# One-hot matrices of 128-column comparisons on VectorE, and their products from block 76 on

## The chip, the cores and the metric

One core of a Trainium2 chip runs the whole kernel. The metric is the device time of one execution in microseconds; the kernel before took 1764.61 us (median of 3 runs). TensorE (PE in the profile), VectorE (DVE), ScalarE (ACT), GpSimd (POOL) and SyncE (SP, which here only issues transfers) run their own instruction streams and wait for each other by semaphores.

## The reference

One transformer block over 512 tokens of width 1024: a conditioned projection, an S5 state-space mixer beside a latent attention, an output projection with a layer norm, and then a feed-forward part by product-key experts, with a second layer norm. The expert part is where the change lies:

```python
def token_block(ht):                                  # 128 tokens at a time
    q = (ht @ w_query).reshape(PEER_BLOCK, PEER_HEADS, PEER_QDIM)
    s1 = einsum('thd,hkd->thk', q[..., :128], keys1)   # 8 heads, 128 keys
    s2 = einsum('thd,hkd->thk', q[..., 128:], keys2)
    v1, i1 = top_k(s1, 16);  v2, i2 = top_k(s2, 16)
    top_s, top_c = top_k(all 256 sums v1 + v2, 16)
    e1 = take_along_axis(i1, top_c // 16);  e2 = take_along_axis(i2, top_c % 16)
    expert = e1 * 128 + e2                             # one of 16384
    g = softmax(top_s)
    act = gelu(einsum('thkd,td->thk', u_tab[expert], ht))
    return einsum('thk,thkd->td', g * act, v_tab[expert])
```

So each token takes 8 x 16 = 128 of 16384 experts, each with a weight g, a row of the table u and a row of the table v, 1024 floats each.

## The kernel before

The parts up to the query scores and the first layer norm end at about 552 us. The rest is the function `experts`, and it has two phases.

**The u phase.** The table u is walked in 128 blocks `b` of 128 experts. For the last 384 tokens every block is multiplied in full: SP loads `u_raw` (512 KB) up to four blocks ahead, ACT copies it to its high half `uth` (L1449, three buffers), POOL subtracts to get the low half `utl` (L1428), and PE runs 24 matmuls of 384 columns (`activations`, L1544 to L1546). ACT applies gelu (`acts`, L1461), and SP stores two blocks at a time to DRAM (`store_acts`, L1358). The first 128 tokens go another way: POOL fetches for each of their 128 chosen experts the row of u of every token (`fetch_rows`, L1423, an indirect transfer of 512 KB into a ring of 8 buffers), and DVE takes the dot product (`use_row`, L1629). `row_steps` writes out at which block POOL issues which fetch; a fetch stands in POOL's stream behind that block's `utl`, and waits until the buffer's last row was used.

**Routing.** While this runs, DVE does the top-k of the four token tiles (`topk`, `routing`), with some `use_row` calls between. A tile's softmax exponentials are done by ACT at written-out blocks (`EXP_AT`: 10, 27, 43, 59). The last tile's route is what the third `route_ready` pair tells.

**The one-hot products.** The 384 tokens need a dense matrix of weights g, 128 experts-by-key-1 by 128 by key 2 for every token. With slots (head, choice) on the partitions, a token's matrix is the product of two one-hot matrices: `hot2[slot, key]` is 1 where key = e2, and `hot1[slot, key]` is the weight where key = e1. The weight is kept as two fp16 numbers, high and low, so that there are `hot2`, `hot1h` and `hot1l`, and two matmuls of 128 columns per token. First PE turns the routes (e1, e2, weight; three 128 x 128 transposes for each of three tiles, L1583) so that slots lie on partitions; this stands ahead of block `HOT_FROM` - 2, and waits for `route_ready`. ACT then copies the weights out of PSUM (L1470, L1471). From block `HOT_FROM` = 64 to `HOT_TO` = 120, PE does 96 groups of 4 tokens (`weights_by_token`, L1559 and L1560), each behind the activations of its block; `block_of(n)` spreads them evenly. ACT copies each group's result to `stage` (L1485), and SP stores every 8 groups (2048 KB, L1363) two blocks later.

The one-hot matrices are made in 24 batches of 16 tokens, two buffers each. A call of `hots(m)` on DVE is three `tensor_tensor` instructions of 2048 columns: `hot_eq` = (iota is e1) at L1735, `hot2` = (iota is e2) at L1736, `hot1l` = `hot_eq` x low weight at L1738; e1, e2 and most of the low weights are read from PSUM (banks 6 and 7). The high part is ACT's: `weigh_high` (L1477), 16 activations of 128 columns per batch with the weight as a per-partition scale. DVE starts batch m when the products of batch m - 2 are done (`g_out`). On DVE each batch is followed by three `use_row` calls:

```python
        for m in range(NBATCH):
            hots(m)
            use_rows(3)
        use_rows(12)
```

**The v phase** starts once block 127 is through: the stored gelu values and weights come back, DVE multiplies them (`w_f`, L1748) and splits them (`wl`, L1753), and PE multiplies with the blocks of the table v (L1568 to L1570). It ends with the second layer norm.

Of the kernel before, what the change touches and what calls it, by code (L numbers as in the profile page):

```python
# [8 lines left out]
F16 = mybir.dt.float16  # L9
# [1084 lines left out]
HOT_FROM, HOT_TO = 64, 120  # L1094
# [5 lines left out]
def place_peer(k):  # L1100
# [45 lines left out]
    k.hot_eq = [k.sb(f"hot_eq{i}", hot, 190 + 4 * i, F16) for i in range(2)]  # L1146
    k.iota_b = k.sb("iota_b", hot, 182, F16)
    k.wT = k.sb("wT", [P, TD], 198)
    k.wTh = k.sb("wTh", [P, TD], 199.5, F16)
    k.wTl = k.sb("wTl", [P, P], 200.5, F16)  # L1150
# [139 lines left out]
def row_steps():  # L1290

    steps = [[] for _ in range(2 * NBLK)]
    for j in range(2 * SLOTS):
        if j < 33:
            at = 14 + 1.4 * j
        elif j < 105:
            at = 59 + (j - 33) * 0.777
        elif j < SLOTS:
            at = 115 + (j - 105) * 0.72
        else:  # L1300
            at = NBLK + 5 + (j - SLOTS) * 0.875
# [4 lines left out]
def experts(nc, io, k, ps, out):  # L1306
# [5 lines left out]
    k.hot_ready, k.eq_ready, k.hot1h_done, k.g_out, k.g_evac = k.sems("hot_ready eq_ready hot1h_done g_out g_evac")  # L1312
# [21 lines left out]
    HOT1H_AT = {}  # L1334
    for m in range(NBATCH):
        for half in range(2):
            HOT1H_AT.setdefault(block_of(PER_BATCH * m) - 2 + half, []).append((m, half))
# [6 lines left out]
    e1_at = [ps[:, 6, t * P:(t + 1) * P] for t in range(DT)]  # L1344
    e2_at = [ps[:, 6, TD:512], ps[:, 7, 0:P], ps[:, 7, P:2 * P]]
    w_low = [ps[:, 7, 2 * P:3 * P], ps[:, 7, 3 * P:4 * P], k.wTl[:, :]]
# [67 lines left out]
    def _(pool):  # L1414
# [11 lines left out]
        for b in range(NBLK):  # L1426
# [5 lines left out]
            if b == G_LAST:  # L1432
                pool.wait_ge(k.hot_ready, NBATCH)
                pool.wait_ge(k.hot1h_done, 2 * NBATCH)
# [13 lines left out]
    def _(act):  # L1448
# [18 lines left out]
        def evacuate_weights():  # L1467
# [3 lines left out]
            nc.scalar.activation(k.wT[:, :], src, ACT.Copy, scale=W_UP).then_inc(k.rt_evac, 1)  # L1471

        def weigh_high(m, half):
            act.wait_ge(k.eq_ready, m + 1)
            for i in range(half * BATCH // 2, (half + 1) * BATCH // 2):
                at = m * BATCH + i
                ins = nc.scalar.activation(k.hot1h[m % 2][:, i], k.hot_eq[m % 2][:, i], ACT.Copy, scale=k.wT[:, at:at + 1])  # L1477
            ins.then_inc(k.hot1h_done, 1)
# [24 lines left out]
        for b in range(NBLK):  # L1503
# [8 lines left out]
            for m, half in HOT1H_AT.get(b, ()):  # L1512
                weigh_high(m, half)
# [22 lines left out]
    def _(pe):  # L1536
# [12 lines left out]
        def weights_by_token(n):  # L1549
            m = n // PER_BATCH  # L1550
            if n % PER_BATCH == 0:
                pe.wait_ge(k.hot_ready, m + 1)
                pe.wait_ge(k.hot1h_done, 2 * m + 2)
# [24 lines left out]
        for b in range(NBLK):  # L1578
            if b == HOT_FROM - 2:
                for t in range(DT):  # L1580
                    pe.wait_ge(k.route_ready, 2 * t + 2)
                    for a, dst in enumerate((e1_at[t], e2_at[t], ps[:, 4, t * P:(t + 1) * P])):
                        ins = nc.tensor.transpose(dst, k.route[:, t + 1, a], k.ident[:, :])  # L1583
# [31 lines left out]
    def _(dve):  # L1615
# [111 lines left out]
        def hots(m):  # L1727
            t, i = divmod(m * BATCH, P)
# [148 lines left out]
```

## Time and profile before

| what | value |
|---|---|
| runs of the kernel before | 1765.5, 1764.61, 1758.7 us; median 1764.61 |
| span of the profiled execution | 1759.0 us |
| its own time | not listed apart; it holds the span and the start and end around it |
| u phase | about 552 to 1190 us |
| v phase and last norm | about 1190 to 1759 us |
| PE / DVE / ACT / POOL busy in the span | 1616.7 / 1335.9 / 721.0 / 1028.7 us |

Times in rows are microseconds from the start of the span unless marked ns. An instruction's duration runs past the start of the next where they are pipelined: two that follow each other without a wait start closer together than they last. "x8" merges eight such instructions, and the duration is then that of all eight. What stands in brackets is the idle time of the engine before the instruction, and what ended it. Blocks can be counted by the stores of `acts`, one for every two blocks (1, 3, 5, ...), the first at 564.55 us.

### The profile page before, as it was taken

The page shows a single profiled execution, that of the slowest core. Times are in us where ns is not written, and L with a number is a line of the kernel's source. Part 1 is how long each engine was busy: PE and PEld are TensorE (multiplying, and loading weights), DVE is VectorE, ACT ScalarE, POOL GpSimd, SP SyncE. Part 2 cuts the span into 40 slices and gives each one's busy share as a digit, 9 for nine tenths or more (in the row PEclk, how much of TensorE's full clock was granted, in tenths as well). Part 3 has the DMA queues.
Part 4 walks back from the last instruction along what each step waited for, and adds up shares of the span by engine and source line. Part 5 has one row for each costly group of instructions (what it writes and reads, how often), then busy time and mean ns, then how long its engine had stood idle before and what let it go on. Part 6 is the DMA issues. An engine that isn't in the chain of part 4 may idle for free.

```text
span 1759.0 us, 22141 instructions
## 1 busy us (share of the span) xinstructions
PE 1616.7 (92%) x8149; PEld 1331.2 (76%) x8149; DVE 1335.9 (76%) x2045; ACT 721.0 (41%) x1249; POOL 1028.7 (58%) x622
## 2 busy tenths in 40 slices
PE   3899999997899999997699999997989999999994
PEld 1345576733789999996699999995878888888883
DVE  2494477227424999999988888827889989998997
ACT  2002122420424424332499999933333333333431
POOL 1500164002003578784577778876879988999863
PEclk9898969998999999998899999998999999999997
DMA  7766200361501477784589999998999999999971
GB/s 252 265 229 109 25 3 1 97 215 48 171 21 58 167 258 253 257 280 152 204 333 356 366 353 334 362 388 316 369 354 370 388 375 369 375 385 375 374 273 48
DMA packets 221974, 436.55 MB, mean 248 GB/s; under 512 B 40893, under 2 KB 135722, under 8 KB 220330
## 3 DMA queue, kind: packets, MB, share of 16 engines
q1 hardware_dynamic: 178410, 299.85, 48.8%
q0 software_dynamic: 36864, 134.23, 21.0%
q10 hardware_dynamic: 6592, 1.05, 0.4%
q8 instruction: 65, 1.06, 0.2%
q14 instruction: 43, 0.35, 0.1%
HBM read 377.28 MB, written 56.62 MB: 247 GB/s over the span
## 4 chain that ended last, share of the span: by engine, by line
PE 28%; DVE 20%; DMA 8%; ACT 7%; issue 4%; SPq 1%; POOL 0%; POOLq 0%; DVEq 0%; ACTq 0%
PE ps L1568 8%; PE ps L1569 8%; PE ps L1570 8%; DMA u_raw<-in_peer_uT 5%; ACT hot1h L1477 3%; ACT stage L1485 2%; DVE junk L1629 2%; DMA a_in<-act_scr 2%; DVE eq L1704 2%; ACT uth L1449 1%; DVE eq L1702 1%; DVE wl L1753 1%; DVE cand L1666 1%; DVE route L1705 1%; DVE idx L1664 1%
## 5 line engine op out<-in xcount | busy, mean ns | idle before, releaser
L1428 POOL TENSOR_TENSOR utl<-u_raw,uth 128x1024 fp32r<-128x1024 f32 x128 | 319.6, 2499 | 225.9 <-ACT uth L1449 224.9
L1544 PE MATMUL ps<-h2h,uth 128*128 128x384 f32 x1024 | 352.3, 344 | 16.2 <-POOL utl L1428 12.2
L1545 PE MATMUL ps<-h2l,uth 128*128 128x384 f32 x1024 | 346.5, 338 | 0.0
L1546 PE MATMUL ps<-h2h,utl 128*128 128x384 f32 x1024 | 346.4, 338 | 0.0
L1438 POOL TENSOR_TENSOR vl<-v_raw,vh 128x1024 fp32r<-128x1024 f32 x128 | 311.2, 2432 | 59.6 <-ACT vh L1449 57.8
L1568 PE MATMUL ps<-vh,wh 128*128 128x512 f32 x768 | 302.1, 393 | 16.2 <-DVE wl L1753 13.5
L1569 PE MATMUL ps<-vl,wh 128*128 128x512 f32 x768 | 301.1, 392 | 0.0
L1570 PE MATMUL ps<-vh,wl 128*128 128x512 f32 x768 | 300.8, 392 | 0.0
L1748 DVE TENSOR_TENSOR w_f<-a_in,g_in 128x384 f32<-128x384 f32 x128 | 208.0, 1626 | 58.6 <-DMA a_in<-act_scr 58.0
L1449 ACT ACTIVATE vh<-v_raw 128x1024 fp32r<-128x1024 f32 x128 | 135.4, 1058 | 217.5 <-DMA v_raw<-in_peer_v 175.4
L1544 PEld LDWEIGHTS ps<-h2h,uth 128*128 128x128 f32 x1024 | 195.6, 191 | 18.1 <-POOL utl L1428 13.8
L1545 PEld LDWEIGHTS ps<-h2l,uth 128*128 128x128 f32 x1024 | 195.6, 191 | 0.0
L1546 PEld LDWEIGHTS ps<-h2h,utl 128*128 128x128 f32 x1024 | 195.4, 191 | 0.0
L1568 PEld LDWEIGHTS ps<-vh,wh 128*128 128x128 f32 x768 | 145.4, 189 | 49.9 <-DVE wl L1753 12.2
L1423 POOL DMA_INDIRECT ring<-in_peer_u,row_at x128 | 145.8, 1139 | 54.1 <-DVE dots L1629 26.3
L1570 PEld LDWEIGHTS ps<-vh,wl 128*128 128x128 f32 x768 | 145.6, 190 | 30.6
L1569 PEld LDWEIGHTS ps<-vl,wh 128*128 128x128 f32 x768 | 145.5, 189 | 30.1
L1637 DVE SCALAR_TENSOR_TENSOR ps<-ring,w_sp,ps 128x1024 f32<-128x1024 f32 x127 | 162.3, 1278 | 2.0 <-DVE ps L1637 0.5
L1629 DVE CUSTOM_DVE_ANT_0 junk<-ring,ps 128x1024 bf16<-128x1024 f32 x128 | 149.9, 1213 | 16.3 <-DMA ring<-in_peer_u,row_at 16.2
L1423 POOL DMA_INDIRECT ring<-in_peer_v,row_at x128 | 138.0, 1078 | 22.4 <-issue 19.9
L1449 ACT ACTIVATE uth<-u_raw 128x1024 fp32r<-128x1024 f32 x128 | 135.2, 1058 | 22.3 <-DMA u_raw<-in_peer_uT 21.4
L1753 DVE TENSOR_TENSOR wl<-w_f,wh 128x384 fp32r<-128x384 f32 x128 | 126.0, 984 | 9.0 <-ACT wh L1449 8.8
(345 smaller groups left out, 2480.2 us busy)
## 6 DMA issues: line engine op xcount, KB each, us to landing
u_raw<-in_peer_uT SPq DMA_DIRECT2D x128, 512.0 KB
v_raw<-in_peer_v SPq DMA_DIRECT2D x128, 512.0 KB
w_ada<-in_w_ada SPq DMA_DIRECT2D x12, 2048.0 KB, 9.8
act_scr<-acts SPq DMA_DIRECT2D x64, 384.0 KB
g_scr<-stage SPq DMA_DIRECT2D x12, 2048.0 KB
g_in<-g_scr SPq DMA_DIRECT2D x32, 768.0 KB
a_in<-act_scr SPq DMA_DIRECT2D x64, 384.0 KB
w_q<-in_peer_w_query SPq DMA_DIRECT2D x8, 1024.0 KB, 6.9
```

Source lines behind the costliest of these rows:

```text
L1423: nc.gpsimd.indirect_dma_start(k.ring[j % RING][:, :], None, table, bass.IndirectOffsetOnAxis(ap=k.row_at[:, slot:slot + 1], axis=0)).then ...
L1428: tt(k.utl[b % 3][:, :, :].rearrange(f3), k.u_raw[:, b % 4].rearrange(f3), k.uth[b % 3][:, :, :].bitcast(F32).rearrange(f3), ALU.subtract) ...
L1438: tt(k.vl[:, n % 4], k.v_raw[:, n % 4], k.vh[:, n % 4].bitcast(F32), ALU.subtract).then_inc(k.vl_done, 1)
L1449: copy = lambda dst, src: nc.scalar.activation(dst, src, ACT.Copy)
L1544: mm(o, hi, k.h2h[:, kt, SP:T], start=(kt == 0), stop=False)
L1545: mm(o, hi, k.h2l[:, kt, SP:T], start=False, stop=False)
L1546: ins = mm(o, lo, k.h2h[:, kt, SP:T], start=False, stop=(kt == DK - 1))
L1568: mm(o, hi, k.vh[:, n % 4, cols], start=(n == 0), stop=False)
L1569: mm(o, hi, k.vl[:, n % 4, cols], start=False, stop=False)
L1570: ins = mm(o, lo, k.vh[:, n % 4, cols], start=False, stop=(n == NBLK - 1))
L1629: ins = v.tensor_tensor_reduce(out=k.junk[j % 2][:, :], in0=row, in1=y_sp, scale=1.0, scalar=0.0, op0=ALU.mult, op1=ALU.add, accum_out=k.d ...
L1748: tt(k.w_f[:, n % 2].rearrange("p (c t) -> p c t", t=CHK), k.a_in[:, p % 2, n % 2].rearrange("p (c t) -> p c t", t=CHK), k.g_in[:, q % 2, ...
```

## The change

DVE makes all three matrices itself, token by token. `hots(m)` becomes 48 `tensor_scalar` instructions of 128 columns: `hot2` compares an fp16 iota row with e2 (one per-partition pointer scalar), `hot1h` and `hot1l` compare it with e1 and multiply by the high-scaled weight or the low weight (two pointer scalars each). The scalars are fp32 columns in SBUF: ACT copies e1 and e2 out of PSUM too, and the low weights are one subtraction over 384 columns. `hot_eq`, the replicated iota, `weigh_high` on ACT and the semaphores between them are gone. `HOT_FROM` is 76: transposes ahead of block 74, ACT's copies at its step 73, 96 product groups in 44 blocks, and with them the 12 stores of `stage`. The row fetches 33 to 104 move from block 59 on (0.777 block apart) to block 73 on (0.611 apart), fetches 105 to 127 from block 115 (0.72 apart) to block 117 (0.66 apart).

```diff
--- before.py
+++ after.py
@@ -1091,7 +1091,7 @@
 BATCH = 16
 GROUPS4 = TD // HOTS
 NBATCH = TD // BATCH
-HOT_FROM, HOT_TO = 64, 120
+HOT_FROM, HOT_TO = 76, 120
 SLOTS = PH * PTOP
 RING = 8
 W_UP = 2.0 ** 14
@@ -1143,11 +1143,12 @@
     k.hot2 = [k.sb(f"hot2{i}", hot, at, F16) for i, at in enumerate((78, 82))]
     k.hot1h = [k.sb(f"hot1h{i}", hot, at, F16) for i, at in enumerate((86, 90))]
     k.hot1l = [k.sb(f"hot1l{i}", hot, at, F16) for i, at in enumerate((94, 98))]
-    k.hot_eq = [k.sb(f"hot_eq{i}", hot, 190 + 4 * i, F16) for i in range(2)]
-    k.iota_b = k.sb("iota_b", hot, 182, F16)
+    k.iota_h = k.sb("iota_h", [P, PKEYS], 182, F16)
+    k.e1T = k.sb("e1T", [P, TD], 182.5)
+    k.e2T = k.sb("e2T", [P, TD], 184)
+    k.wTl = k.sb("wTl", [P, TD], 185.5)
     k.wT = k.sb("wT", [P, TD], 198)
     k.wTh = k.sb("wTh", [P, TD], 199.5, F16)
-    k.wTl = k.sb("wTl", [P, P], 200.5, F16)
     k.stage = k.sb("stage", [P, 2, PKEYS, CHK], 110)
 
 
@@ -1294,9 +1295,9 @@
         if j < 33:
             at = 14 + 1.4 * j
         elif j < 105:
-            at = 59 + (j - 33) * 0.777
+            at = 73 + (j - 33) * 0.611
         elif j < SLOTS:
-            at = 115 + (j - 105) * 0.72
+            at = 117 + (j - 105) * 0.66
         else:
             at = NBLK + 5 + (j - SLOTS) * 0.875
         steps[int(at)].append(j)
@@ -1309,7 +1310,7 @@
     k.w_done, k.wh_done, k.wl_done, k.vh_done, k.vl_done = k.sems("w_done wh_done wl_done vh_done vl_done")
     k.y_mm, k.y_done = k.sems("y_mm y_done")
     k.route_ready, k.rt_out, k.rt_evac, k.exp6_in, k.exp6_done = k.sems("route_ready rt_out rt_evac exp6_in exp6_done")
-    k.hot_ready, k.eq_ready, k.hot1h_done, k.g_out, k.g_evac = k.sems("hot_ready eq_ready hot1h_done g_out g_evac")
+    k.hot_ready, k.g_out, k.g_evac = k.sems("hot_ready g_out g_evac")
     k.gcol2_ready, k.gate2_out, k.gate2_evac = k.sems("gcol2_ready gate2_out gate2_evac")
     k.h_sp, k.rows_at, k.row_used, k.gelu_sp, k.w_sp_ready = k.sems("h_sp rows_at row_used gelu_sp w_sp_ready")
     k.s_x1b, k.s_ln2, k.s_out, k.y_norm, k.y_ready = k.sems("s_x1b s_ln2 s_out y_norm y_ready")
@@ -1331,19 +1332,12 @@
     for n in range(GROUPS4):
         GROUPS_AT.setdefault(block_of(n), []).append(n)
     STORE_AT = {block_of(PER_CH * ch + PER_CH - 1) + 2: ch for ch in range(NCH)}
-    HOT1H_AT = {}
-    for m in range(NBATCH):
-        for half in range(2):
-            HOT1H_AT.setdefault(block_of(PER_BATCH * m) - 2 + half, []).append((m, half))
     G_LAST = HOT_TO
     LAST4 = NBLK - 4
     DOTS_END, SP_GELU, SP_WEIGH = 8, 9, 11
     f3 = "p k n -> p (k n)"
     BANK = dict(zip([(t, half) for t in range(DT) for half in range(2)], (4, 5, 6, 7, 2, 3)))
     y_sp = ps[:, 0:2].rearrange("p a n -> p (a n)")
-    e1_at = [ps[:, 6, t * P:(t + 1) * P] for t in range(DT)]
-    e2_at = [ps[:, 6, TD:512], ps[:, 7, 0:P], ps[:, 7, P:2 * P]]
-    w_low = [ps[:, 7, 2 * P:3 * P], ps[:, 7, 3 * P:4 * P], k.wTl[:, :]]
     u_rows, v_rows = io["peer_u"][0], io["peer_v"][0]
     ROWS_AT = row_steps()
 
@@ -1431,7 +1425,6 @@
                 fetch_rows(j)
             if b == G_LAST:
                 pool.wait_ge(k.hot_ready, NBATCH)
-                pool.wait_ge(k.hot1h_done, 2 * NBATCH)
                 nc.gpsimd.tensor_copy(k.gcol2[:, :, :], k.modc[:, 5 * DK:6 * DK].unsqueeze(2).broadcast_to([P, DK, P])).then_inc(k.gcol2_ready, 1)
         for n in range(NBLK):
             pool.wait_ge(k.vh_done, n + 1)
@@ -1468,14 +1461,9 @@
             act.wait_ge(k.rt_out, DT)
             src = ps[:, 4, 0:TD]
             nc.scalar.activation(k.wTh[:, :], src, ACT.Copy, scale=W_UP)
-            nc.scalar.activation(k.wT[:, :], src, ACT.Copy, scale=W_UP).then_inc(k.rt_evac, 1)
-
-        def weigh_high(m, half):
-            act.wait_ge(k.eq_ready, m + 1)
-            for i in range(half * BATCH // 2, (half + 1) * BATCH // 2):
-                at = m * BATCH + i
-                ins = nc.scalar.activation(k.hot1h[m % 2][:, i], k.hot_eq[m % 2][:, i], ACT.Copy, scale=k.wT[:, at:at + 1])
-            ins.then_inc(k.hot1h_done, 1)
+            nc.scalar.activation(k.wT[:, :], src, ACT.Copy, scale=W_UP)
+            copy(k.e1T[:, :], ps[:, 6, 0:TD])
+            copy(k.e2T[:, :], ps[:, 7, 0:TD]).then_inc(k.rt_evac, 1)
 
         def evacuate_g(n):
             ch, at = n // PER_CH, n % PER_CH * HOTS
@@ -1509,8 +1497,6 @@
                 evacuate_weights()
             for n in GROUPS_AT.get(b - 1, ()):
                 evacuate_g(n)
-            for m, half in HOT1H_AT.get(b, ()):
-                weigh_high(m, half)
             if b == G_LAST + 2:
                 act.wait_ge(k.gate2_out, 1)
                 for half in range(2):
@@ -1550,7 +1536,6 @@
             m = n // PER_BATCH
             if n % PER_BATCH == 0:
                 pe.wait_ge(k.hot_ready, m + 1)
-                pe.wait_ge(k.hot1h_done, 2 * m + 2)
             if n >= 2:
                 pe.wait_ge(k.g_evac, n - 1)
             for j in range(HOTS):
@@ -1579,8 +1564,8 @@
             if b == HOT_FROM - 2:
                 for t in range(DT):
                     pe.wait_ge(k.route_ready, 2 * t + 2)
-                    for a, dst in enumerate((e1_at[t], e2_at[t], ps[:, 4, t * P:(t + 1) * P])):
-                        ins = nc.tensor.transpose(dst, k.route[:, t + 1, a], k.ident[:, :])
+                    for a, bank in enumerate((6, 7, 4)):
+                        ins = nc.tensor.transpose(ps[:, bank, t * P:(t + 1) * P], k.route[:, t + 1, a], k.ident[:, :])
                     ins.then_inc(k.rt_out, 1)
             activations(b)
             if b == HOT_FROM:
@@ -1725,17 +1710,16 @@
                 step(ins)
 
         def hots(m):
-            t, i = divmod(m * BATCH, P)
-            at = slice(i, i + BATCH)
             if m >= 2:
                 dve.wait_ge(k.g_out, (m - 1) * PER_BATCH)
-                dve.wait_ge(k.hot_ready, m - 1)
-            iota, eq = k.iota_b[:, :, :], k.hot_eq[m % 2][:, :, :]
-            e1, e2, wl = (a[t][:, at].unsqueeze(2).broadcast_to([P, BATCH, PKEYS]) for a in (e1_at, e2_at, w_low))
-            tt(eq, iota, e1, ALU.is_equal).then_inc(k.eq_ready, 1)
-            tt(k.hot2[m % 2][:, :, :], iota, e2, ALU.is_equal)
-            dve.wait_ge(k.eq_ready, m + 1)
-            tt(k.hot1l[m % 2][:, :, :], eq, wl, ALU.mult).then_inc(k.hot_ready, 1)
+            iota = k.iota_h[:, :]
+            for i in range(BATCH):
+                at = m * BATCH + i
+                e1, e2, w, wl = (a[:, at:at + 1] for a in (k.e1T, k.e2T, k.wT, k.wTl))
+                v.tensor_scalar(k.hot2[m % 2][:, i], iota, e2, None, ALU.is_equal)
+                v.tensor_scalar(k.hot1h[m % 2][:, i], iota, e1, w, ALU.is_equal, ALU.mult)
+                ins = v.tensor_scalar(k.hot1l[m % 2][:, i], iota, e1, wl, ALU.is_equal, ALU.mult)
+            ins.then_inc(k.hot_ready, 1)
 
         def weight(n):
             p, q = n // 2, n // 4
@@ -1759,12 +1743,9 @@
             rows = (2, 2, 2, 3, 2)
             topk(it, rows)
             routing(it, rows)
-        v.tensor_copy(k.iota_b[:, :, :], k.iota[:, :].unsqueeze(1).broadcast_to([P, BATCH, PKEYS]))
+        v.tensor_copy(k.iota_h[:, :], k.iota[:, :])
         dve.wait_ge(k.rt_evac, 1)
-        for t in range(DT):
-            at = slice(t * P, (t + 1) * P)
-            ins = tt(w_low[t], k.wT[:, at], k.wTh[:, at], ALU.subtract)
-        step(ins)
+        step(tt(k.wTl[:, :], k.wT[:, :], k.wTh[:, :], ALU.subtract))
         for m in range(NBATCH):
             hots(m)
             use_rows(3)
```

## Rows read from the trace of the kernel before

**Rows 1.** stretches: us, busy time by engine, granted clock, DMA share, GB/s
```profile
core 0: us, PE busy (x) PEld busy (x) DVE busy (x) ACT busy (x) POOL busy (x), PEclk, DMA share, GB/s
834.00:854.00 20.00, 6.19 (x29) 5.92 (x29) 19.66 (x18) 0.10 (x1) 9.38 (x5) 0.67 0.47 170
865.00:1155.00 290.00, 283.83 (x2118) 272.45 (x2117) 246.10 (x222) 270.49 (x575) 220.69 (x131) 1.00 0.93 350
1155.00:1190.00 35.00, 33.58 (x198) 32.94 (x196) 7.56 (x14) 11.84 (x17) 22.97 (x15) 1.00 1.00 381
```

**Rows 2.** timeline of SyncE's queue, stores of acts: start us, us
```profile
635.55 0.38 SPq L1358 DMA_DIRECT2D act_scr<-acts  x1
...
643.87 0.38 SPq L1358 DMA_DIRECT2D act_scr<-acts  x1
...
876.29 0.38 SPq L1358 DMA_DIRECT2D act_scr<-acts  x1
...
1153.24 0.38 SPq L1358 DMA_DIRECT2D act_scr<-acts  x1
```

**Rows 3.** timeline of TensorE around block 62
```profile
838.45 0.82 PE L1583 MATMUL ps<-ident,route 128*128 128x128 f32 x6
853.08 0.90 PE L1583 MATMUL ps<-ident,route 128*128 128x128 f32 x3 [13.81 <-DVE route L1719]
```

**Rows 4.** timeline of ScalarE, the gelu of block 118
```profile
1147.65 0.49 ACT L1461 ACTIVATE acts<-ps 128x384 f32<-128x384 f32 x1 [1.77 <-PE ps L1546]
```

**Rows 5.** VectorE groups, 900 to 1150 us: busy us, mean ns, idle
```profile
L1629 DVE CUSTOM_DVE_ANT_0 junk<-ring,ps 128x1024 bf16<-128x1024 f32 x65 | 75.8, 1213 | 5.7 <-DMA ring<-in_peer_u,row_at 5.7
L1735 DVE TENSOR_TENSOR hot_eq<-iota_b,ps 128x2048 f16<-128x2048 f16 x20 | 45.7, 2287 | 31.9 <-PE ps L1560 31.5 <-issue 0.4
...
L1738 DVE TENSOR_TENSOR hot1l<-hot_eq,ps 128x2048 f16<-128x2048 f16 x12 | 27.4, 2279 | 0.0
```

**Rows 6.** waits from 870 to 1200 us: total us, times, longest
```profile
DVE hot_eq L1735 <- PE ps L1560: 34.9, 17, 4.8
```

**Rows 7.** timeline of VectorE, one-input instructions without pointer scalars
```profile
23.86 0.43 DVE L316 TENSOR_SCALAR rtmp<-rtmp 128x512 f32<-128x512 f32 x1
24.21 0.42 DVE L317 TENSOR_SCALAR ang<-ang 128x512 f32<-128x512 f32 x1
...
597.40 0.22 DVE L1695 TENSOR_SCALAR cab<-topc 128x128 uint32<-128x128 uint32 x1
597.53 0.22 DVE L1696 TENSOR_SCALAR cab<-topc 128x128 uint32<-128x128 uint32 x1
```

**Rows 8.** timeline of VectorE, with one pointer scalar, then with two
```profile
329.02 1.67 DVE L983 TENSOR_SCALAR y_mla<-y_mla,rstd 128x512 f32<-128x512 f32 x4
...
69.33 3.74 DVE L367 TENSOR_SCALAR hT<-hT,modc 128x512 f32<-128x512 f32 x8
```

**Rows 9.** timelines of VectorE and GpSimd at the same moments, twice
```profile
833.02 2.29 DVE L1695 TENSOR_SCALAR cab<-topc 128x128 uint32<-128x128 uint32 x1
...
832.85 2.38 POOL L1428 TENSOR_TENSOR utl<-u_raw,uth 128x1024 fp32r<-128x1024 f32 x1 [0.81 <-ACT uth L1449]
...
750.45 3.19 DVE L1698 CAST cabf<-cab 128x256 f32<-128x256 uint32 x1
...
750.09 0.96 POOL L1423 DMA_INDIRECT ring<-in_peer_u,row_at  x1
751.07 2.40 POOL L1428 TENSOR_TENSOR utl<-u_raw,uth 128x1024 fp32r<-128x1024 f32 x1
```

**Rows 10.** GpSimd groups from 900 to 1150 us
```profile
L1428 POOL TENSOR_TENSOR utl<-u_raw,uth 128x1024 fp32r<-128x1024 f32 x48 | 115.3, 2401 | 47.6 <-ACT uth L1449 47.2
L1423 POOL DMA_INDIRECT ring<-in_peer_u,row_at x63 | 75.3, 1195 | 11.7 <-issue 6.2 <-DVE dots L1629 1.4
```

**Rows 11.** transfers from 900 to 1150 us
```profile
DMA packets 23638, 89.56 MB, mean 358 GB/s; under 512 B 2285, under 2 KB 8305, under 8 KB 22209
```

## The prediction

> **What bounds the kernel now.** I read the table of stretches first. From 865 to 1155 us, where the products stand in, PE is busy for 283.83 of 290 us at full clock, ACT for 270.49, DVE for 246.10, and the DMA engines for 93% [rows 1]. So four resources are near their end there, and PE sets the pace. The stores of `acts` give it: two blocks took 8.32 us before the products, 4.16 each; from block 65 to block 119 it was 1153.24 - 876.29 = 276.95 us for 54 blocks, 5.13 each [rows 2]. The 0.97 more are 96/56 = 1.71 product groups, 0.57 us each.
>
> The second view is TensorE's timeline. Its first six transposes ran at 838.45; the last three waited 13.81 us for the last route, until 853.08 [rows 3], and in the stretch around it PE is busy 31% of the time at a mean clock of 0.67 [rows 1]. That is the stall that a later `HOT_FROM` can take away.
>
> The third is DVE's table of groups. A batch costs it three one-hot instructions of 2.28 to 2.29 us and three dot products of 75.8/65 = 1.17 us, 3.5 in all [rows 5]: 10.4 us. It has 56/24 = 2.33 blocks for that, 12.0 us. The waits agree: DVE stood for 34.9 us in all until a product was done [rows 6]. DVE has 1.6 us to spare per batch, no more, and that is the number to watch.
>
> **The change part by part.** *ACT.* 16 activations per batch go, two copies come. ACT is busy 93% of the stretch, but PE 98% [rows 1], so this alone gains little. Its cover: ACT becomes free work time that nobody waits for. Priced at nothing.
>
> *The later start.* The 13.81 us wait goes, as block 62 now needs no route. PE would begin block 62's activations at 838.5 and reach block 74 at 838.5 + 12 x 4.16 = 888. From the last transposes (853.08) to the first one-hot instruction it was 2.6 us; six more transposes and two copies make about 4. The first batch starts at 892. Meanwhile DVE, done with the route at about 853 as before, stands idle for some 37 us that it used for batches.
>
> *DVE's cost per token.* The trace has no 128-column fp16 instruction with one input, so I bound it. Two instructions without pointers start 0.35 us apart at 512 fp32 columns, and 0.13 apart at 128 uint32 columns; the first lasts 0.43, so 0.08 overlaps the next [rows 7]. That is 0.57 ns per column, 0.073 for 128, and 0.057 fixed. Four 512-column instructions with one pointer scalar took 1.67 us, eight with two pointers 3.74 [rows 8]: less the 0.08, that is 0.398 and 0.458 each, so the first pointer adds 0.048 us and both add 0.108. A token then costs, at 4-byte speed, 0.178 + 2 x 0.238, and 16 tokens 10.5 us. If 2-byte columns stream in half the time, it is 0.142 + 2 x 0.202, or 8.7 us. If streaming cost nothing it would be 7.0; if the columns went at the 2.29/2048 us of the old one-hot instruction [rows 5], 13.7. I take 9.6, the middle of the two likely ones; the ends are 7.0 and 13.7. The old batch was 6.9 on the same engine: the change takes DVE more time, since 48 instructions pay the fixed part and 80 pointers.
>
> *GpSimd in the way.* One-input DVE instructions between SBUF tiles don't run while POOL subtracts: a 128-column instruction that otherwise takes 0.22 lasted from 833.02 for 2.29 us, to the moment at which `utl` (832.85, 2.38) was through; a cast at 750.45 lasted 3.19, over the rest of a row fetch and the whole of a `utl` [rows 9]. The old one-hot instructions, with an input in PSUM, kept to 2.28 [rows 5]. In a new batch time POOL does 44/24 = 1.83 `utl` of 2.40 us, 4.4 in all, and three fetches of about 1.2, 3.6 in all [rows 10]. The dot products read PSUM and can run beside them. The least that falls on the one-hots is 4.4 - 3.5 = 0.9 us, the most 8.0, and nothing if the lock doesn't touch such short instructions. A fetch waits for a row that was used, so the fetches and one `utl` will mostly run beside the dot products. I take the other 0.83 `utl`, 2.0 us, and a quarter of the fetches, 0.9: 2.9 us.
>
> *The batch time.* T = 9.6 + 3.5 + 2.9 = 16.0 us. PE needs only 1.83 x 4.16 + 4 x 0.57 = 9.9 us for the same batch. So DVE becomes the bound of all 24 batches, and PE waits for it about 6 us in each. The last batch is ready at 892 + 24T - 3.5. Its products stand behind the activations of block 118, which before ended at 1147.65 [rows 4]; what follows is the same nine blocks in both. The change in time is then 892 + 24T - 3.5 - 1147.6 = 24T - 259 us. At T = 16.0 that is +125. It is zero at T = 10.8.
>
> *The moved transfers.* u blocks stay; 12 stores of 2048 KB are issued on SP in 44 blocks instead of 56, and 72 fetches on POOL in 44 instead of 56. Per block: 0.524 MB of u, 0.197 of `acts`, 0.524/0.611 = 0.858 of rows, 12 x 2.097/44 = 0.572 of `stage`, 2.15 MB. The chip moved 358 GB/s over the old products [rows 11] and 381 when it was full [rows 1], so a block can't take less than 5.65 us. With T = 16.0 a block takes 8.7, and transfers are hidden. SP's store of `stage` would wait longer for its group, with u loads behind it, but those are four blocks ahead. After block 118 less is queued, which may give back up to 5 us; I count none.
>
> *The sum.* 1759.0 + 125 = 1884 us of span. The median is 5.6 above the profiled span, so 1890.
>
> The halving for 2-byte columns is the step that no row shows. The Trainium skill, page "VectorE: DVE Perf Modes", section "The perf-mode tier table", says that a one-source instruction on 2-byte SBUF data goes four columns per cycle and fp32 two. By it the batch is the 8.7 us case, T = 15.1 and the time 1868; by 4-byte speed it is T = 16.9 and 1911.
>
> **The rivals.** *B: the lock doesn't bite.* Short instructions slip between POOL's, or POOL's work falls beside the dot products and PE's stalls. T = 13.1, +55 us, 1820. Against it: both examples of rows 9.
>
> *C: one column at a time.* The two-operator form with pointers may stream no faster than the old one-hots: 13.7 + 3.5 = T of 17.2 with no lock, +154, 1918. Nothing shows it, but nothing shows a fast fp16 one either.
>
> *D: faster.* The pointers are fetched while the instruction before runs, and a batch of 48 takes 7.0 us or less. The price decides at T = 10.8, that is 7.3 us per batch or 0.152 us per instruction. Then the transfers bound the stage: 42 blocks of 5.65 us from the end of block 76's activations (838.5 + 15 x 4.16 = 901) end block 118 at 1138, 10 us earlier than before; if they went at PE's 5.4 us, at 1128, 20 us earlier. That is 1745 to 1755. For it: the stall of rows 3 is real. Against: in rows 8 the pointers cost time in instructions that stood back to back.
> The Trainium skill, same page, section "The TRN2 errata", gives 58 cycles plus the columns over the speed-up for a VectorE instruction, with no term for pointers. By it 128 columns would be (58 + 32)/0.96 = 94 ns, an estimate, a batch 4.5 us, and case D would come true. By that rule 512 fp32 columns take 0.33 us, and rows 7 have 0.35; but rows 8 stand 0.05 and 0.11 above rows 7.
>
> *E: no change* needs T between 10.4 and 11.2.
>
> *F: the clock.* PE idle for 6 us per batch may be granted the half clock, as around the old stall [rows 1]. At half speed throughout a batch would need 19.8 us of PE, and PE would bound. But it would then not be idle. I leave it inside the upper end of the forecast.
>
> **How the numbers follow.** A, the forecast with its lock, 0.62: T from 14.0 to 18.0, so +77 to +173, 1842 to 1938. B 0.12, C 0.14, D 0.08, E 0.04. 0.5% (8.8 us) is about what a measurement of this kernel can tell from no change. D is faster by more than that, E within it, the rest slower: 0.08, 0.04, 0.88. The range runs from just under B, 1812, to 1950, above C and the forecast's own end; out of it are D, E and a lock that costs all of the 8.0 us.
>
> **What would show it.** In the profile after: `tensor_scalar` starts 0.15 (one pointer) and 0.2 us (two) apart where POOL is quiet, and single ones of up to 2.4 us where it isn't; no wait of PE for the route at L1583; PE waiting for DVE's one-hots some 24 times, 5 to 7 us each; DVE busy all through the stage; stores of `acts` 16 to 18 us apart; ACT well under half busy; DMA at 60 to 70%. The forecast is wrong if the 48 instructions take under 7.3 us with dot products left at 3.5, or if PE isn't the one who waits.

## The result and the profile after

The changed kernel took 1912.65 us (median of 4 runs, 1908.1 to 1917.0), the kernel before 1762.39 in the same runs: 1.084 times as long, with an interval of 1.081 to 1.087. The profiled span is 1915.2 us. The forecast was 1890 us, case A.

The table of stretches of the changed kernel, over the two stretches that [rows 1] has of before:

```profile
core 0: us, PE busy (x) PEld busy (x) DVE busy (x) ACT busy (x) POOL busy (x), PEclk, DMA share, GB/s
834.00:854.00 20.00, 19.18 (x96) 19.21 (x97) 19.83 (x16) 7.25 (x11) 12.06 (x5) 0.84 0.58 182
865.00:1155.00 290.00, 210.88 (x1337) 203.35 (x1336) 260.63 (x829) 110.34 (x134) 136.15 (x90) 0.84 0.65 228
```

The old stall is gone: from 834 to 854 us PE is busy for 19.18 us instead of 6.19. Where the products stand it is turned round. PE fell from 283.83 busy microseconds to 210.88, ACT from 270.49 to 110.34, DMA from 93% to 65%, and DVE rose to 260.63 (it is idle up to 895). The granted clock fell from 1.00 to 0.84, in a stretch in which PE now pauses in every batch.

The stores of `acts` of blocks 79 and 119 on SyncE's queue:

```profile
939.91 0.38 SPq L1352 DMA_DIRECT2D act_scr<-acts  x1
...
1307.62 0.38 SPq L1352 DMA_DIRECT2D act_scr<-acts  x1
```

That is 367.7 us for 40 blocks, 9.2 each, where [rows 2] gave 5.13. The waits of the changed kernel from 870 to 1320 us:

```profile
POOL ring L1417 <- DVE dots L1614: 192.2, 24, 9.9
...
PE ps L1544 <- DVE hot1l L1721: 121.4, 24, 9.2
...
DVE wTl L1748 <- ACT e2T L1442: 30.5, 1, 30.5
```

PE waits for the last one-hot instruction in each of the 24 batches, 5.1 us on the mean. GpSimd waits for dot products, and DVE waited once, 30.5 us, for ScalarE's copies of the route: the idle time that the late start brings (the forecast had some 37). What DVE does, in its own timeline (L1719 is `hot2`, with one pointer scalar; L1720 and L1721 are `hot1h` and `hot1l`, with two; L1614 is the dot product):

```profile
894.93 0.26 DVE L1719 TENSOR_SCALAR hot<-iota_h,e2T 128x128 f16<-128x128 f16 x1
...
1003.28 0.24 DVE L1719 TENSOR_SCALAR hot<-iota_h,e2T 128x128 f16<-128x128 f16 x1
1003.45 0.30 DVE L1720 TENSOR_SCALAR hot1h<-iota_h,e1T,wT 128x128 f16<-128x128 f16 x1
1003.67 0.30 DVE L1721 TENSOR_SCALAR hot1l<-iota_h,e1T,wTl 128x128 f16<-128x128 f16 x1
1003.89 0.24 DVE L1719 TENSOR_SCALAR hot<-iota_h,e2T 128x128 f16<-128x128 f16 x1
...
1011.20 1.22 DVE L1614 CUSTOM_DVE_ANT_0 junk<-ring,ps 128x1024 bf16<-128x1024 f32 x1
...
1014.62 0.09 DVE L1614 DVE_READ_ACCUMULATOR2_ANT dots<- 128x1 f32 x1
...
1016.63 3.00 DVE L1720 TENSOR_SCALAR hot1h<-iota_h,e1T,wT 128x128 f16<-128x128 f16 x1
...
1020.16 0.53 DVE L1721 TENSOR_SCALAR hot1l<-iota_h,e1T,wTl 128x128 f16<-128x128 f16 x1
...
1028.30 1.21 DVE L1614 CUSTOM_DVE_ANT_0 junk<-ring,ps 128x1024 bf16<-128x1024 f32 x1
...
1299.06 0.30 DVE L1721 TENSOR_SCALAR hot1l<-iota_h,e1T,wTl 128x128 f16<-128x128 f16 x1
1299.29 1.21 DVE L1614 CUSTOM_DVE_ANT_0 junk<-ring,ps 128x1024 bf16<-128x1024 f32 x1
```

Three things are to be read there. Undisturbed starts follow each other by 0.17, 0.22 and 0.22 us; from 1003.28 to 1010.59, the `hot2` starts of twelve tokens apart, it is 0.609 us per token, 9.74 per batch. One period, from dot product to dot product, is 1028.30 - 1011.20 = 17.1 us. And from 894.93 to 1299.29 there are 24 batches with 23 sets of dot products: with one more set of 3.4 us, 24T = 407.8, so T = 17.0 us. GpSimd's timeline in the same period shows the rest, 17.0 - 9.7 - 3.4 = 3.9 us:

```profile
1012.70 0.94 POOL L1417 DMA_INDIRECT ring<-in_peer_u,row_at  x1 [9.94 <-DVE dots L1614]
1013.66 2.38 POOL L1422 TENSOR_TENSOR utl<-u_raw,uth 128x1024 fp32r<-128x1024 f32 x1
1016.20 0.96 POOL L1417 DMA_INDIRECT ring<-in_peer_u,row_at  x1 [0.16 <-issue]
1017.16 2.41 POOL L1422 TENSOR_TENSOR utl<-u_raw,uth 128x1024 fp32r<-128x1024 f32 x1
```

The subtraction from 1013.66 to 1016.04 began under the dot products, and held the one-hot of 1014.62 for its last 1.4 us. The next ran from 1017.16 to 1019.57, and the one-hot of 1016.63, issued in a row fetch just ahead of it, lasted 3.00 us, until it was over. A fetch alone moved no start: the one-hot of 1020.16 has a duration of 0.53 instead of 0.30 us, but the next one starts at 1020.38, 0.22 later as always. Over the whole stage, 45 of the 1152 one-hot instructions were held for over 0.4 us, and each of them met a subtraction; 212 met only a fetch, and the starts behind them came no later. All hold-ups together are 3.8 us per batch.

### The profile page after: what moved, and what is told of

It reads as the page before. It is cut to its first block, busy times and chain, and to the rows that moved or that the text cites. A ratio compares the mean times of both kernels' runs of the same rounds, so it can differ in the third digit from the quotient of the medians.

```text
span 1915.2 us, 22814 instructions
## 1 busy us (share of the span) xinstructions
PE 1666.9 (87%) x8149; PEld 1380.9 (72%) x8149; DVE 1509.8 (79%) x3123; ACT 620.6 (32%) x867; POOL 1009.8 (53%) x622
## 4 chain that ended last, share of the span: by engine, by line
DVE 40%; PE 12%; issue 9%; DMA 7%; POOL 2%; SPq 1%; ACT 1%; POOLq 0%; DVEq 0%; ACTq 0%
DVE hot1h L1720 6%; DVE hot L1719 6%; DVE hot1l L1721 5%; DVE junk L1614 4%; DMA v_raw<-in_peer_v 4%; DMA a_in<-act_scr 3%; PE ps L1553 2%; PE ps L1554 2%; PE ps L1555 2%; DVE ps L1622 2%; DVE wl L1737 2%; PE ps L1530 1%; PE ps L1531 1%; PE ps L1532 1%; POOL vl L1431 1%
## 5 line engine op out<-in xcount | busy, mean ns | idle before, releaser
L1530 PE MATMUL ps<-h2h,uth 128*128 128x384 f32 x1024 | 365.8, 357 | 19.5 <-ACT acts L1454 17.0
L1531 PE MATMUL ps<-h2l,uth 128*128 128x384 f32 x1024 | 358.2, 350 | 0.0
L1532 PE MATMUL ps<-h2h,utl 128*128 128x384 f32 x1024 | 357.1, 349 | 0.0
L1732 DVE TENSOR_TENSOR w_f<-a_in,g_in 128x384 f32<-128x384 f32 x128 | 219.0, 1712 | 44.9 <-DMA a_in<-act_scr 37.6
L1417 POOL DMA_INDIRECT ring<-in_peer_u,row_at x128 | 128.4, 1003 | 222.9 <-DVE dots L1614 195.9
L1530 PEld LDWEIGHTS ps<-h2h,uth 128*128 128x128 f32 x1024 | 207.1, 202 | 20.4 <-issue 17.6
L1531 PEld LDWEIGHTS ps<-h2l,uth 128*128 128x128 f32 x1024 | 206.1, 201 | 0.0
L1454 ACT ACTIVATE acts<-ps 128x384 f32<-128x384 f32 x128 | 62.9, 491 | 348.3 <-PE ps L1532 340.2
L1544 PE MATMUL ps<-hot1h,hot 128*128 128x128 f16 x384 | 64.7, 257 | 123.1 <-DVE hot1l L1721 121.4
L1614 DVE CUSTOM_DVE_ANT_0 junk<-ring,ps 128x1024 bf16<-128x1024 f32 x128 | 149.5, 1211 | 15.0 <-DMA ring<-in_peer_u,row_at 14.9
L1720 DVE TENSOR_SCALAR hot1h<-iota_h,e1T,wT 128x128 f16<-128x128 f16 x384 | 151.5, 395 | 0.0
```

The lines of the kernel that those rows point to most:

```text
L1530: mm(o, hi, k.h2h[:, kt, SP:T], start=(kt == 0), stop=False)
L1531: mm(o, hi, k.h2l[:, kt, SP:T], start=False, stop=False)
L1532: ins = mm(o, lo, k.h2h[:, kt, SP:T], start=False, stop=(kt == DK - 1))
L1614: ins = v.tensor_tensor_reduce(out=k.junk[j % 2][:, :], in0=row, in1=y_sp, scale=1.0, scalar=0.0, op0=ALU.mult, op1=ALU.add, accum_out=k.d ...
L1720: v.tensor_scalar(k.hot1h[m % 2][:, i], iota, e1, w, ALU.is_equal, ALU.mult)
L1732: tt(k.w_f[:, n % 2].rearrange("p (c t) -> p c t", t=CHK), k.a_in[:, p % 2, n % 2].rearrange("p (c t) -> p c t", t=CHK), k.g_in[:, q % 2, ...
```

## The experiments

In e7, e8 and e10 the last exponentials stand at ScalarE's step 64; in all others they stand at 59, as in both kernels. The time before was 1762.4 to 1765.4 us in each set of runs.

**Form alone (e1).** The changed kernel with the start of before:

```diff
-HOT_FROM, HOT_TO = 76, 120
+HOT_FROM, HOT_TO = 64, 120
```
(and the old two rates of `row_steps`.)

> The changed kernel with the old start: products from block 64, the old schedule of row fetches, the new one-hot instructions. My theory is that the time of a batch on VectorE decides: 48 instructions that take 9.7 us alone (0.165 us with one pointer scalar, 0.2225 with two, in the trace after), 3.4 us of dot products, and what GpSimd's work holds up, 3.9 us of the 17.0 measured. Now there are 2.33 blocks in a batch, not 1.83, so some 1.2 us more of GpSimd's subtractions fall in it: T = 18.2 us. The first batch starts about 37 us earlier. Last batch ready near 858 + 24 x 18.2 - 3.4 = 1291 instead of 1299, with one block more behind it: about 1908 us, at most 15 us from the changed kernel. The rival, that the loss comes from the later start and from products, stores and fetches squeezed into 44 blocks, expects 1765 +- 20.

Measured: 1913.93 us, ratio 1.085 (1.083 to 1.088). The start can be undone and nothing comes back. With the new instructions the loss is all there. In the trace the first one-hot starts at 859.5 and the 24th batch at 1280.5, so T is 18.3 us: the batches start 35 us earlier, and 24 times 1.3 us more takes that back.

**Start alone (e2).** The kernel before with `HOT_FROM` = 76 and the new rates of `row_steps`, `tensor_tensor` one-hots and `weigh_high` untouched.

> The kernel before with the new start alone: products from block 76 and the new schedule of row fetches, the old one-hot instructions on VectorE and ScalarE. My theory: a batch costs VectorE 10.4 us, TensorE 9.9, the transfers 10.4, and ScalarE 16 x 0.30 + 4 x 1.0 + 1.83 x 1.5 = 11.6, so ScalarE bounds at 11.6; the last batch is ready near 895 + 24 x 11.6 - 3 = 1170, where the kernel before had block 118 at 1148: about +20, 1783 us (1765 to 1800). The rival, that the late start is what costs, expects 1880 or more.

Measured: 1843.31 us, ratio 1.047 (1.043 to 1.050). This fits neither: 60 us over my number, 78 over the time before. Its waits from 840 to 1260 us:

```profile
POOL utl L1428 <- ACT uth L1449: 157.2, 55, 9.4
PE ps L1559 <- ACT stage L1485: 76.7, 30, 9.0
DVE hot_eq L1735 <- PE ps L1560: 74.4, 19, 9.4
...
ACT hot1h L1477 <- DVE hot_eq L1735: 61.8, 17, 7.2
```

The last three of these waits close a ring. ACT stood 61.8 us at its one-hot activations for `hot_eq`; DVE stood 74.4 us (the kernel before: 34.9, [rows 6]) for products of PE, which free the buffer; PE stood 76.7 us for ACT's copies to `stage`, which come behind the activations in ACT's stream.

**The ring (e5).** To the kernel of e2, one edit:

```diff
-            HOT1H_AT.setdefault(block_of(PER_BATCH * m) - 2 + half, []).append((m, half))
+            HOT1H_AT.setdefault(block_of(PER_BATCH * m) - 1 + half, []).append((m, half))
```

> The kernel of the start alone (old one-hots, products from block 76) lost 78 us where I had expected 20. Its trace has ScalarE waiting at its one-hot activations for VectorE, VectorE for TensorE's products of the batch before the last, and TensorE for ScalarE's copy of the last group. ScalarE does its half batches in order, two blocks and one block ahead of the batch's first products, and a batch now lasts 1.83 blocks, so it comes to stand before products that free the buffers it waits for. Theory: that ring of waits is the loss. Here the half batches stand one block ahead and at the block itself, and nothing else is changed: ScalarE's own 11.6 us per batch bound again, 1785 us (1770 to 1800). The rival, that the transfers squeezed into 44 blocks or the later start itself cost the 78 us, expects 1843 as before.

Measured: 1793.29 us, ratio 1.017 (1.015 to 1.020). 50 us came back by moving ACT's half batches one block (47 if each kernel is set against the time before of its own set). So the ring was the larger part of the 78 us.

**The iota in PSUM (e3).** The changed kernel, reading its iota row as fp32 from PSUM:

```diff
-        v.tensor_copy(k.iota_h[:, :], k.iota[:, :])
         dve.wait_ge(k.rt_evac, 1)
+        v.tensor_copy(ps[:, 7, 3 * P:4 * P], k.iota[:, :])
...
-            iota = k.iota_h[:, :]
+            iota = ps[:, 7, 3 * P:4 * P]
```

> The changed kernel with the iota row as fp32 in PSUM instead of fp16 in SBUF. If GpSimd holds up instructions only where they take both SBUF ports, the single instructions of 2.4 to 3 us go (3.9 us per batch), but each of the 48 streams one column at a time, about 0.1 us more: 14.6 + 3.4 = 18.0 us per batch with no waits for GpSimd, +24 us: about 1937. If the hold-up has nothing to do with the ports, single instructions of 2.4 us stay, T is near 22 us and the time 2030.

Measured: 1932.99 us, ratio 1.097 (1.093 to 1.101). The summary of the two-pointer instruction (duration min/median/max in ns), and VectorE's timeline:

```profile
L1720 DVE TENSOR_SCALAR hot1h<-ps,e1T,wT x384: 401/962/1357, 895.5 to 1316.6; 128x128 f16<-128x128 f32 x192
```

```profile
1001.50 0.63 DVE L1719 TENSOR_SCALAR hot<-ps,e2T 128x128 f16<-128x128 f32 x1
1001.76 0.69 DVE L1720 TENSOR_SCALAR hot1h<-ps,e1T,wT 128x128 f16<-128x128 f32 x1
1002.08 0.69 DVE L1721 TENSOR_SCALAR hot1l<-ps,e1T,wTl 128x128 f16<-128x128 f32 x1
1002.40 0.63 DVE L1719 TENSOR_SCALAR hot<-ps,e2T 128x128 f16<-128x128 f32 x1
```

No instruction of the 384 lasted over 1.36 us: none was held for a subtraction of 2.4 us. The starts are 0.26, 0.32 and 0.32 apart, 0.90 per token or 14.4 per batch, and with 3.4 T is 17.8. From the span (1931.4 against 1915.2) it is 17.0 + 16.2/24 = 17.7. The hold-ups of 3.8 us per batch are gone, and 4.7 us of slower streaming took their place. So the hold-up goes with an SBUF input of this one-input form. The edit changes the type together with the place; that the 2-byte type isn't what GpSimd holds up is seen in [rows 9], where the held instruction reads uint32 from SBUF. Which of the two makes the streaming slower isn't told apart. (The durations of 0.6 us and more beside starts 0.3 apart are overlap; the starts are what counts.)

**Pointers (e4).** The changed kernel with constants for e1, e2 and both weights, so that its one-hot matrices don't depend on the routes:

```diff
-                v.tensor_scalar(k.hot2[m % 2][:, i], iota, e2, None, ALU.is_equal)
+                v.tensor_scalar(k.hot2[m % 2][:, i], iota, float(i), None, ALU.is_equal)
```
(and `float(i + 1)` with 100.0 or 0.01 in the other two.)

> The changed kernel with constants in place of the pointer scalars in the 48 instructions, so that the one-hot matrices don't depend on the routes (the output is not the reference's). If the pointers cost what the rows before showed (0.048 for the first, 0.108 for two), a batch is 16 x 0.264 = 4.2 us shorter, 12.8 us, and the time 24 x 4.2 = 101 us less: about 1811. If pointers are free and the fixed part is all, it stays at 1912. If TensorE bounded the stage, it would stay too.

Measured: 1805.47 us, ratio 1.023 (1.020 to 1.025). VectorE's timeline:

```profile
998.39 2.43 DVE L1719 TENSOR_SCALAR hot<-iota_h 128x128 f16<-128x128 f16 x1
1000.74 0.18 DVE L1720 TENSOR_SCALAR hot1h<-iota_h 128x128 f16<-128x128 f16 x1
1000.84 0.18 DVE L1721 TENSOR_SCALAR hot1l<-iota_h 128x128 f16<-128x128 f16 x1
1000.95 0.18 DVE L1719 TENSOR_SCALAR hot<-iota_h 128x128 f16<-128x128 f16 x1
```

The starts are 0.10 us apart, 4.9 per batch instead of 9.7, and an instruction that meets a subtraction still lasts 2.43. The time fell by 107 us, 4.5 per batch; T in the trace is 12.4 (24th batch at 1179.0, the first at 892.9). The instructions gave 4.8, and the hold-ups, 4.1 instead of 3.8, took 0.3 back. One pointer costs 0.165 - 0.102 = 0.063 us, two 0.12.

**Another form for all one-hots on VectorE (e6, e7).** The instructions are four `tensor_tensor` again, with the tokens innermost, so that every operand is fp16 at step one:

```diff
-    hot = [P, BATCH, PKEYS]
+    hot = [P, PKEYS, BATCH]
...
+            e1, e2, w, wl = (a[:, at].unsqueeze(1).broadcast_to([P, PKEYS, BATCH]) for a in (k.e1T, k.e2T, k.wTh, k.wTl))
+            tt(eq, iota, e1, ALU.is_equal).then_inc(k.eq_ready, 1)
+            tt(k.hot2[m % 2][:, :, :], iota, e2, ALU.is_equal)
+            dve.wait_ge(k.eq_ready, m + 1)
+            tt(k.hot1h[m % 2][:, :, :], eq, w, ALU.mult)
+            tt(k.hot1l[m % 2][:, :, :], eq, wl, ALU.mult).then_inc(k.hot_ready, 1)
```

> All one-hots on VectorE and none on ScalarE, as in the changed kernel, products from block 64 as before, but in four tensor_tensor instructions of 2048 columns per batch, with the tokens innermost so that all operands are fp16 at step one in SBUF. If such an instruction takes half of the old 2.28 us, a batch is 4 x 1.14 + 3.4 = 8.0 us plus at most 3 for GpSimd, less than the 12.0 of 2.33 blocks; TensorE and the transfers bound as before: 1750 to 1765 us. If it takes 2.2 us, T is near 12.2 + 3 = 15 and the time 1830. TensorE then reads its one-hot operands with a step of 32 bytes; if that slows a matmul of 128 columns from 0.06 to 0.2 us, 768 of them cost 100 us. The theory that the form (many short instructions with pointers) is the loss, and not the absence of ScalarE, needs this kernel to be far below 1912.

Measured: 1925.67 us, ratio 1.092 (1.089 to 1.094). VectorE's timeline and TensorE's, from e6:

```profile
1019.15 3.09 DVE L1719 TENSOR_TENSOR hot_eq<-iota_h,e1T 128x2048 f16<-128x2048 f16 x1 [15.42 <-PE ps L1546]
1022.16 1.21 DVE L1720 TENSOR_TENSOR hot<-iota_h,e2T 128x2048 f16<-128x2048 f16 x1
1023.29 1.21 DVE L1722 TENSOR_TENSOR hot1h<-hot_eq,wTh 128x2048 f16<-128x2048 f16 x1
```

```profile
1002.20 0.42 PE L1545 MATMUL ps<-hot1h,hot 128*128 128x128 f16 x1
1002.44 0.42 PE L1546 MATMUL ps<-hot1l,hot 128*128 128x128 f16 x1
1002.67 0.42 PE L1545 MATMUL ps<-hot1h,hot 128*128 128x128 f16 x1
```

The first half of the guess held: the instructions start 1.13 us apart (the first was held by GpSimd). The other half failed by the risk that I had named: matmuls of 128 columns whose operands are read with a step of 32 bytes stand 0.24 us apart, not 0.056. 768 of them make 141 us of the 163 that were lost; the mean clock from 865 to 1155 us was 0.92 instead of 1.00 besides. PE was busy for all 290 us of that stretch and waited for nobody. The kernel says nothing about VectorE's part, then.

> The same one-hots with the products from block 71, the last exponentials at ScalarE's step 64 instead of 59, and the row fetches from block 68 (0.68 apart). The wait of some 20 us at block 59 for the exponentials and the 13.8 us at block 62 both go, since the route is ready when TensorE reaches block 69, near 853 us instead of block 62. A batch has 2.04 blocks, 10.5 us. If the one-hots take less than that, 1735 us (1725 to 1760); if the transfers can't go faster, no gain over the version from block 64.

Measured: 1912.34 us, ratio 1.085 (1.082 to 1.088). The same price hides what the start gives; it was only 13 us better than e6.

**Pairs (e9).** Only two tokens are interleaved:

```diff
-    hot = [P, PKEYS, BATCH]
+    hot = [P, BATCH // 2, PKEYS, 2]
```
(and the operands indexed to match.)

> Tokens innermost made VectorE fast (four instructions of 1.13 us per batch) but the matmuls of 128 columns, read with a step of 32 bytes, stood 0.24 us apart instead of 0.056. Here only two tokens are interleaved, so TensorE reads with a step of 4 bytes, and VectorE's operands are still fp16 at step one. Products from block 64, as before. If VectorE keeps its 1.13 us and the step of 4 bytes costs TensorE nothing, the batch is bound by TensorE and the transfers as before: 1750 to 1765 us. If a pair at a time halves nothing for VectorE: four times 2.2 us, T near 14, 1815 us. If TensorE reads at half speed, 768 x 0.056 = 43 us more: 1800 us. The theory that ScalarE's one-hots weren't what the changed kernel lacked, and that its instruction form is, needs 1765 or less.

Measured: 1755.52 us, ratio 0.996 (0.995 to 0.998). TensorE's group of one-hot matmuls from 900 to 1140 us (before had 332 from 900 to 1150, at a mean of 221 ns too), and one instruction of VectorE:

```profile
L1545 PE MATMUL ps<-hot1h,hot 128*128 128x128 f16 x326 | 43.4, 221 | 0.0
```

```profile
1009.26 3.42 DVE L1723 TENSOR_TENSOR hot1h<-hot_eq,wTh 128x2048 f16<-128x2048 f16 x1
```

A step of 4 bytes costs TensorE nothing: the matmuls start 0.057 us apart, and 0.056 in the kernel before. All one-hots are on VectorE, none on ScalarE, as the change wanted, and the loss is gone. GpSimd's hold-ups are not gone: an instruction that otherwise takes 1.21 us lasts up to 3.4. But four instructions 1.13 us apart and three dot products make 7.9 us, so that they fit into the batch: T is 11.6, and PE waits for VectorE once, 1.0 us, from 865 to 1140 us.

**Pairs with the changed kernel's own start (e11).** e9 with `HOT_FROM` = 76 and the new `row_steps`. It differs from the changed kernel in the form of VectorE's instructions alone, with the tile layouts that go with it.

> The one-hots in interleaved pairs with exactly the start and the row fetches of the changed kernel (products from block 76, exponentials at step 59). It differs from the changed kernel in the form of VectorE's instructions alone. My account says that with a quick VectorE the late start costs nothing: the 13.8 us wait for the route is gone and the transfers bound at 5.65 us per block, so block 118 ends near 1138, 10 us before the old time: 1745 us with the same end (1735 to 1765). If the late start has a price of its own, apart from the two rings of waits seen so far, it is 1775 or more.

Measured: 1766.23 us, ratio 1.001 (0.9998 to 1.003). The table of stretches:

```profile
900.00:1150.00 250.00, 231.17 (x1770) 222.39 (x1769) 225.57 (x243) 151.97 (x178) 219.36 (x117) 0.97 0.95 361
```

The form alone is worth 1912.65 - 1766.23 = 146 us. The start costs 11 us against e9, where I had expected a gain of 10. From block 76 to block 118 a block took 5.87 us instead of 5.65. From 900 to 1150 us PE stood 18.8 us, all of it for ACT's copies to `stage`, and ACT stood 14.5 us for the landing of `u_raw`; PE's two longest waits (3.71 us at 969.00 and 4.23 at 1098.78) stand right behind ACT's of 2.06 and 2.56. At 361 GB/s and 95% the transfers are then the likely bound. That is argued from these waits; the rate varied from 326 to 388 GB/s between stretches of 50 us.

**A better start (e8, e10).** Both kernels have a stall that the later start doesn't touch. At its step 59 ScalarE waits for VectorE's top scores of the last tile before it can do the exponentials, first in the kernel before, then in the changed one:

```profile
829.72 0.31 ACT L1465 ACTIVATE tops<-tops 128x128 f32<-128x128 f32 x1 [20.37 <-DVE tops L1692]
```

```profile
832.56 0.31 ACT L1458 ACTIVATE tops<-tops 128x128 f32<-128x128 f32 x1 [15.79 <-DVE tops L1677]
```

ScalarE's copies for the next blocks stand behind them, and PE of the changed kernel waited 12.6 us there. So e8 (the old one-hots, with ScalarE's half batches one block later as in e5) and e10 (the pairs) have products from block 71, row fetches 33 to 104 from block 68 (0.68 block apart), and the last exponentials five steps later:

```diff
-        EXP_AT = {10: 0, 27: 1, 43: 2, 59: 3}
+        EXP_AT = {10: 0, 27: 1, 43: 2, 64: 3}
```

> The old one-hots with the same start at block 71, the exponentials at step 64, the fetches from block 68, and ScalarE's half batches one block later. ScalarE needs 4.8 + 4.0 + 2.04 x 1.5 = 11.9 us per batch, so the last batch is ready near 857 + 24 x 11.9 = 1143, 5 us before the old time: 1760 us (1750 to 1785). Against the tokens-inner kernel it shows what ScalarE's part costs.

Measured: 1753.27 us, ratio 0.994 (0.992 to 0.996).

> The same one-hots with the start that served the old form best: products from block 71, the last exponentials at step 64, fetches from block 68. The old form took 1753 us there, with ScalarE at 11.9 us per batch as the bound I had named. Without ScalarE's part a batch is bound by TensorE, 2.04 x 4.16 + 4 x 0.57 = 10.8 us, and the transfers, about 10.9: 24 us less than at 11.9. 1740 us (1725 to 1755). If ScalarE was not the bound, 1753.

Measured: 1730.17 us, ratio 0.982 (0.980 to 0.983). The table of stretches of e10:

```profile
834.00:854.00 20.00, 19.79 (x117) 19.52 (x115) 19.80 (x17) 8.47 (x11) 15.85 (x7) 1.00 0.71 233
865.00:1140.00 275.00, 273.23 (x2067) 264.20 (x2065) 251.02 (x257) 174.09 (x206) 248.66 (x133) 1.00 0.98 372
```

PE has no stall from 834 to 854 us (4.8 us are left, at 858.6, for the last route), and is busy for 273.23 of the 275 us in which the products stand. This kernel beats both. Against e8 it is 23 us faster, and T is 10.5 instead of 11.4: that is what the old form costs at this start. The forecast for e8 had named ScalarE's part as its bound, at 11.9; as e8 and e10 differ in VectorE's instructions too, that it is ScalarE is argued.

## Why the prediction was right

*VectorE becomes the bound.* Right. T was forecast as 16.0 and is 17.0; PE waits 24 times, 5.1 us each (forecast: about 6). e3 and e4 move T by +0.8 and -4.5, and the span followed 24 times that within 3 us (+16 and -110). In e1 T is 18.3 and the start 35 us earlier; together that makes -3, and the span changed by -4.

*The instructions.* Forecast 9.6 us per batch, measured 9.7, but by two errors that cancel. The rows gave 0.048 and 0.108 us for the pointers; they cost 0.063 and 0.12. The rest of an instruction was put between 0.094 and 0.13 us and is 0.10. By the 2-byte rule of the Trainium skill, page "VectorE: DVE Perf Modes", section "The perf-mode tier table", the batch would have been 8.7 with the pointers of [rows 8]; with the measured ones it is 9.4. Case D had the formula of the same page, section "The TRN2 errata", beside it: 94 ns, an estimate. e4 comes near it, at 102 ns, once no pointer is there. What it leaves out is the pointers, 4.9 of 9.7 us per batch. They don't decide the sign alone: e4 has none and is still 2.3% slower, as GpSimd's hold-ups bring its T to 12.4, above the 10.8 at which the change is zero.

*GpSimd in the way.* The mechanism was right, the size was the term that was off: 2.9 us forecast, 3.9 in the period shown (3.8 on the mean), 24 us of the 31 by which the span missed. I had one subtraction run beside the dot products. In the period shown only 0.96 us of it did: the first fetch is released by the first dot product, so GpSimd's work starts when little of the dot products is left. The fetches, which I had put at 0.9, cost next to nothing.

*The rest of the miss.* The first batch started at 894.9, not 892, as the exponentials at step 59 came 2.8 us later than in the kernel before; what follows the last batch took 1915.2 - 1299.3 = 615.9 us instead of 1759.0 - 1147.6 = 611.4. 24 + 3 + 4 is the 31.

*The later start.* The stall of [rows 3] went as forecast, and gave nothing while VectorE bounds: e1 and the changed kernel agree. Two terms that had no say here were wrong. Pricing ScalarE's one-hots at nothing overlooked that in the old form they can't follow to block 76 without the ring of e2. And the least time of a block was put too low (e11). The waits for the exponentials at step 59, which a later `HOT_FROM` leaves as they are, were not looked at; e10 took them away together with most of the wait for the route.

*The rivals.* B: the lock bites, as e3 shows by its absence. C: the columns stream fast; C needed 0.143 us for the columns of one instruction (which makes its batch 13.8, not 13.7 us), and in e4 whole instructions start 0.102 us apart. The time alone couldn't have told C from the forecast: C's 1918 lies nearer to the measured 1912.65 than the forecast's 1890, and so does the 1911 of columns at 4-byte speed, both by luck. D: no, a batch takes 9.7 us and not 7.3; and D priced no hold-ups, so that its 7.3 was too kind a limit (e4, at 4.9, still loses). F: the clock fell to 0.84 and PE's own part of a batch grew from 9.9 to 11.7 us (281.87 us busy from 895 to 1300, over 24), and it still had 5 us to spare in each.

What stays open: e6 reads both matmul operands with the large step, so which of the two is slow isn't told apart. In e3 the place and the type of the iota changed together. Of the 31 us that e5 still loses I expected 20; the other 11 are about what the same start costs in e11, where the transfers were the likely bound, but that they are the same is argued, not shown.

## What to carry to other kernels

Before work moves to an engine, sum its period with the new work in it and compare that with the period of the engine that sets the pace; a busy share of 85% left 1.6 us here, and the change took 6.6, hold-ups included. Count short instructions by their start-to-start time, with a term for each pointer scalar, and add the time for which another engine's work holds them up; here a subtraction of GpSimd did, unless it ran beside the dot products. If a one-hot or another broadcast comparison has to be fast, interleave just two columns so that all operands are 2-byte at step one, and keep the step at which TensorE reads small. When a stage is compressed, look at each written-out lead against the new length of a batch.

## What was not expected of the hardware

- A pointer scalar costs VectorE 0.063 us, two cost 0.12, in instructions that otherwise start 0.102 us apart.
- A row fetch of GpSimd (0.95 us) alone moved no start of a one-hot, though it made one duration 0.23 us longer (1020.16); a subtraction held it to its end.
- With the iota as fp32 in PSUM, 128 columns took 0.09 to 0.10 us more, and nothing was held.
- TensorE reads 128-column fp16 operands at a step of 4 bytes as fast as dense ones, at 32 bytes four times slower (0.24 against 0.056 us).
- A `tensor_tensor` of 2048 fp16 columns, all operands in SBUF, starts 1.13 us before the next when the innermost step of each is one (e6, e9). In the kernel before, `hot1l` with a broadcast low weight in SBUF starts 2.20 us before the next where nothing holds it.
